# A two-block transformer on one Trainium2 core: a merged attention stage spread over more units, and two weight splits placed earlier

## The chip, the core and the metric

The kernel runs on one core of one Trainium2 chip. The time is device microseconds from start to end of one execution. Before the change three executions took 2884.49, 2887.8 and 2883.33 us; their median is 2884.49 us. The core has a matrix engine (TensorE, PE in the profile), a vector engine (VectorE, DVE), a scalar engine (ScalarE, ACT), GpSimd (POOL) and SyncE (SP), which here only issues transfers. Each engine works through its own instructions in the order in which they are written, and engines wait for each other with semaphores. PSUM, where PE writes, has eight banks of 128 x 512 numbers.

## The reference, cut to what matters

The program is one pass of a network over 512 tokens of width 1024: two attention layers with their feed-forward parts, then a block with a recurrent mixer, a cross attention and a mixture of 32 experts. Three places matter here.

```
# even_mixer: two attentions over the same tokens, 8 heads each
logits = q @ k.T * scale                       # MLA heads, causal
p = softmax(where(mask, logits, -1e30)); out = p @ v
z = q @ k.T * scale                            # stick-breaking heads
log_beta, log_1m = log_sigmoid(z), where(mask, log_sigmoid(-z), 0)
suffix = cumsum_from_the_right(log_1m) - log_1m
a = where(mask, exp(log_beta + suffix), 0); out = a @ v
# hybrid_mixer: proj = xn @ w_in, then for its first 2048 columns
qk = silu(causal_depthwise_conv(qk, conv_w, conv_b))      # 4 taps
# hierarchical_moe, for each block of rows of one expert
hb = silu(xb @ w1[e]) * (xb @ w3[e]); out = hb @ w2[e]
```

## The kernel before

**High and low parts.** The large products take each fp32 number as two: a rounded high part, which ACT writes by a copy (L324; L2319 for the experts), and the rest, which DVE writes by a subtraction (L330; L2324). PE then runs three matmuls for each pair of tiles (L305 to L307, or L2351 to L2353). Weights arrive in a ring of buffers and are split in pieces of 128 x 2048, one ahead of the other; `w_hi` and `x_hi` count ACT's halves, `w_lo` and `x_lo` those of DVE. A piece is written into one of two places (four for the experts), so a split waits until PE has used the piece before in that place.

**The merged attention (stage `two_pe`, `two_act`, `two_dve`, `two_po`).** A unit is one head and one block of 128 queries; its row of scores has 128, 256, 384 or 512 columns (`causal`), and 8 heads give 32 units. Both kinds of attention run their 32 units side by side, one of each per turn of a loop over v. For an MLA unit: scores (L1423), maximum (L974) and its scaling (L1022), exp (L942), transposes of the weights (L897), ACT copy (L925), value product (L907), scaling and store (L952, L954); at two of a head's four units PE also transposes the next head's q or k (L879) and ACT copies it (L918). For a stick unit: scores (L1450), three ACT steps abs, exp and ln (L1478 to L1480, `b_t1`), DVE's softplus (L1515, `b_sp`), a mask on POOL (L1523), DVE's running sum and a subtraction (L1509, L1511, `b_w`), a second mask (L1529), exp (L1485), transposes (L1458), copy (L1492), value product (L1468, `b_o`), and DVE's copy out of the bank (L1499, `b_on`). Only one PSUM bank holds stick value products, so the next one waits for that copy out. A score bank is free again once its unit's subtraction is done (`b_w`). What stands in turn v on each engine, by unit, is written in the loops of the four functions and is the order in which the engines execute.

**The mixer's input (stage `mp_pe`, `mp_act`, `mp_dve`).** PE computes 16 chunks of 128 columns, four per weight matrix (`qkj`); a matrix comes in two pieces. PE first runs all four chunks over piece one, then over piece two. DVE runs the convolution of a chunk in five steps (L1784, L1785, L1787 three times), ACT the silu (L1754). `msp.before` splits a first piece of the next matrix, `msp.after` its second piece: before the change, after the fourth chunk of each matrix.

**The experts (stage `ex_pe`, `ex_act`, `ex_dve`).** 32 experts, each with six pieces of weights (1 MB each). PE multiplies rows with w1 and w3 (`up`), DVE forms the gated product (L2407), PE transposes it (`turn`, L2378), ACT writes the high part (L2413) and DVE the low part (L2417) of the transposed rows, and PE multiplies with w2 (`down`). PE's order is: `up` of the next expert, first half; `turn`; `up`, second half; `down`; `up` with w3. DVE's list for one expert is six piece splits q = p to p+5 with the gated product after the first and the low part (`turned_low`) after the third. SP reloads one of five weight buffers when both splits of its matrix are done (L2669).

Of the kernel before, what the change touches and what calls it, by code (L numbers as in the profile page):

```python
# [33 lines left out]
P = 128  # L34
S = 512
NT = S // P
# [76 lines left out]
def bass_two_blocks_kernel(nc, I, out):  # L113
# [11 lines left out]
    with ctx:  # L125
# [711 lines left out]
        class Attention:  # L837
# [73 lines left out]
            def act(self, act, v):  # L911
                units = self.units
# [6 lines left out]
                if 2 <= v < units + 2:  # L919
                    u = v - 2  # L920
# [5 lines left out]
                if v < units:  # L926
# [243 lines left out]
        if on(1):  # L1170
# [255 lines left out]
            def scale_mla(v):  # L1426
# [5 lines left out]
                            score_banks=(0, 1), turn_banks=(2,), value_banks=(6,), prep_bank=2)  # L1432
# [5 lines left out]
            def sb_bank(v):  # L1438
                return ps[:, 3 + v % 2, 0:causal(v)]
# [4 lines left out]
            def sb_pe(pe, v):  # L1444
                if v < U0:
                    h, i = divmod(v, NT)
                    if v >= 2:
                        pe.wait_ge(b_w, v - 1)
# [3 lines left out]
                if 3 <= v < U0 + 3:  # L1452
                    u = v - 3
# [6 lines left out]
                if 4 <= v < U0 + 4:  # L1460
                    u = v - 4
# [10 lines left out]
            def sb_act(act, ch, v):  # L1472
                if v < U0:
                    act.wait_ge(b_sc, v + 1)
                    if v >= 4:
                        act.wait_ge(b_w, v - 3)
                    t1 = T1[:, v % 4, 0:causal(v)]
                    ch(act.activation(t1, sb_bank(v), ACT.Abs))  # L1478
                    ch(act.activation(t1, t1, ACT.Exp, scale=-1.0))
                    act.activation(t1, t1, ACT.Ln, bias=1.0).then_inc(b_t1, 1)  # L1480
                if 2 <= v < U0 + 2:
                    u = v - 2
# [3 lines left out]
                if 3 <= v < U0 + 3:  # L1486
                    u = v - 3
# [1242 lines left out]
```

## Time and profile before

| | value |
|---|---|
| median of three executions | 2884.49 us (2883.33 to 2887.8) |
| the profiled execution | 2887.3 us, its span 2885.6 us |
| PE busy | 2657.8 us (92%) |
| DVE busy | 1522.2 us (53%) |
| ACT busy | 1234.1 us (43%) |
| POOL busy | 122.6 us (4%) |
| TensorE clock granted, mean | 0.939 |
| DMA | 432.84 MB, mean 150 GB/s |

Busy shares are over the whole span, and the span consists of stages that follow one another. The merged attention lies at 144 to 311 us, the mixer's input at about 1453 to 1605 us, the experts at about 2240 to 2847 us. A row of the timeline gives the start, the length, the engine, the line, the operation, what is written and read, the shapes, the count, and in square brackets the idle time before it with the instruction that ended it. Neighbouring rows of an engine overlap by some 0.1 us where nothing has to be waited for, so times are taken from start to start. A clock of 1.00 is 2.4 GHz, 0.50 is 1.2 GHz.

### The profile page before, as it was taken

What the parts mean: (1) busy time and instruction counts of PE and PEld (TensorE: products, weight loads), DVE (VectorE), ACT (ScalarE), POOL (GpSimd) and SP (SyncE); (2) the same over time, 40 slices, a digit from 0 to 9 for tenths busy, and PEclk for the clock granted to TensorE, in tenths of its full rate; (3) what the DMA queues carried; (4) which work ended last, traced back from release to release, by engine and by line L of the source; (5) the groups of instructions that cost most, each with busy time, mean ns of one, the idle gap of its engine ahead of it and who ended that gap; (6) DMA issues with size and microseconds to landing.
All of it is one profiled execution on the core that took longest, in us unless ns stands there. A gap on an engine that the chain in (4) does not pass through costs nothing. (4 is left out here: it accounts for less than half of the span.)

```text
span 2885.6 us, 30599 instructions
## 1 busy us (share of the span) xinstructions
PE 2657.8 (92%) x12110; PEld 2158.0 (75%) x12110; DVE 1522.2 (53%) x2085; ACT 1234.1 (43%) x1570; POOL 122.6 (4%) x166
## 2 busy tenths in 40 slices
PE   6998999999998999999989969798995899999994
PEld 5866778888887777888877658677874777877774
DVE  4555444344323654434466443245346788888884
ACT  3366432223334742213222222324242677777773
POOL 0111000000140000000000000000002000000001
PEclk9967799999998999999989989899997899999997
DMA  3300132433431023342322022221304899999993
GB/s 130 119 1 1 50 120 93 139 109 119 138 110 37 1 76 116 108 146 88 117 88 88 30 95 88 73 88 59 142 14 190 345 392 396 395 396 396 396 392 119
DMA packets 157146, 432.84 MB, mean 150 GB/s; under 512 B 11051, under 2 KB 80838, under 8 KB 144582
## 3 DMA queue, kind: packets, MB, share of 16 engines
q1 hardware_dynamic: 148950, 400.90, 38.1%
q10 hardware_dynamic: 4608, 16.78, 1.4%
q0 software_dynamic: 3440, 13.11, 1.3%
q8 instruction: 102, 1.67, 0.2%
q14 instruction: 46, 0.38, 0.0%
HBM read 383.58 MB, written 47.19 MB: 149 GB/s over the span
## 5 line engine op out<-in xcount | busy, mean ns | idle before, releaser
L307 PE MATMUL ps<-area,area 128*128 128x512 f32 (+1 forms) x1696 | 658.5, 388 | 0.0
L330 DVE TENSOR_TENSOR area<-area,area 128x2048 fp32r<-128x2048 f32 (+4 forms) x161 | 340.5, 2117 | 598.5 <-ACT area L324 598.5
L306 PE MATMUL ps<-area,area 128*128 128x512 f32 (+5 forms) x1432 | 552.0, 385 | 0.0
L324 ACT ACTIVATE area<-area 128x2048 fp32r<-128x2048 f32 (+4 forms) x161 | 284.1, 1767 | 615.6 <-PE ps L307 582.4
L2324 DVE TENSOR_TENSOR area<-area,area 128x2048 fp32r<-128x2048 f32 x192 | 433.9, 2286 | 107.3 <-ACT area L2319 107.3
L305 PE MATMUL ps<-actT_parts,area 128*128 128x512 f32 x968 | 385.4, 398 | 11.6 <-DVE area L330 9.4
L306 PE MATMUL ps<-actT_parts,area 128*128 128x512 f32 x968 | 383.3, 396 | 0.0
L2319 ACT ACTIVATE area<-area 128x2048 fp32r<-128x2048 f32 x192 | 361.0, 1913 | 48.5 <-PE ps L2353 18.4
L307 PEld LDWEIGHTS ps<-area,area 128*128 128x128 f32 x1696 | 320.4, 189 | 68.3
L306 PEld LDWEIGHTS ps<-area,area 128*128 128x128 f32 x1432 | 277.5, 194 | 52.8
L305 PE MATMUL ps<-area,actT_parts 128*128 128x512 f32 (+3 forms) x704 | 274.6, 390 | 39.6 <-DVE area L330 30.8
L305 PE MATMUL ps<-area,area 128*128 128x512 f32 (+2 forms) x728 | 277.4, 381 | 9.3 <-DVE area L694 9.3
L307 PE MATMUL ps<-area,actT_parts 128*128 128x512 f32 (+3 forms) x704 | 274.0, 389 | 0.0
L305 PEld LDWEIGHTS ps<-actT_parts,area 128*128 128x128 f32 x968 | 183.0, 189 | 57.6 <-DVE area L330 10.3
L306 PEld LDWEIGHTS ps<-actT_parts,area 128*128 128x128 f32 x968 | 182.8, 189 | 42.3 <-issue 1.2
L2351 PE MATMUL ps<-area,actT_parts 128*128 128x512 f32 x512 | 205.9, 402 | 0.0
L2353 PE MATMUL ps<-area,actT_parts 128*128 128x512 f32 x512 | 203.4, 397 | 0.0
L2352 PE MATMUL ps<-area,actT_parts 128*128 128x512 f32 x512 | 203.2, 397 | 0.0
L305 PEld LDWEIGHTS ps<-area,actT_parts 128*128 128x128 f32 x704 | 139.7, 198 | 70.3 <-issue 39.1
L305 PEld LDWEIGHTS ps<-area,area 128*128 128x128 f32 x728 | 137.7, 189 | 35.7 <-issue 10.2
L307 PEld LDWEIGHTS ps<-area,actT_parts 128*128 128x128 f32 x704 | 139.7, 198 | 26.7
L907 PE MATMUL ps<-area,area 128*128 128x64 f32 (+1 forms) x624 | 111.3, 313 | 15.9 <-DVE actT L954 9.3
(329 smaller groups left out, 3205.3 us busy)
## 6 DMA issues: line engine op xcount, KB each, us to landing
area<-in_w SPq DMA_DIRECT2D x96, 2048.0 KB, 10.1
area<-in_w_in SPq DMA_DIRECT2D x16, 2048.0 KB, 7.9
area<-in_l_w_gate SPq DMA_DIRECT2D x22, 1024.0 KB, 5.4
area<-in_l_w_up SPq DMA_DIRECT2D x22, 1024.0 KB, 8.0
expert_inputs<-maskz SPq DMA_DIRECT2D x39, 512.0 KB, 8.7
area<-in_l_w_in SPq DMA_DIRECT2D x9, 2048.0 KB, 8.2
area<-expert_inputs SPq DMA_DIRECT2D x32, 512.0 KB, 9.7
expert_rows<-area ACTq DMA_DIRECT2D x32, 512.0 KB, 8.6
```

The lines of the kernel that those rows point to most:

```text
L305: pe.matmul(dst(r), a.h, b.h, start=begin, stop=False)
L306: pe.matmul(dst(r), a.l, b.h, start=False, stop=False)
L307: m = pe.matmul(dst(r), a.h, b.l, start=False, stop=end)
L324: eng.activation(w.h, raw, ACT.Copy).then_inc(w_hi, 1)
L330: dve.tensor_tensor(w.l, raw, w.high_f, ALU.subtract).then_inc(w_lo, 1)
L907: m = pe.matmul(self.value_at(u), self.PT[:, u % 2, j * P:j * P + P], self.values(u, j), start=(j == 0), stop=(j == nb - 1))
L2319: act.activation(w.h, raw, ACT.Copy).then_inc(x_hi, 1)
L2324: dve.tensor_tensor(w.l, raw, w.high_f, ALU.subtract).then_inc(x_lo, 1)
L2351: pe.matmul(dst, a.h, b.h, start=first, stop=False)
L2352: pe.matmul(dst, a.l, b.h, start=False, stop=False)
L2353: return pe.matmul(dst, a.h, b.l, start=False, stop=last)
```

## The change

Three edits.

1. In the merged attention the MLA scores have one bank instead of two, the stick scores three instead of two. The steps of a unit are spread over more turns, and each engine's turn is put in another order. On PE the stick scores are computed one unit ahead, and the stick value product moves to the end of the turn. On DVE the running sum belongs to the unit two turns back and stands first in the turn, the softplus to the unit one turn back, and the copy out of the value bank stands last. On ACT the abs, exp and ln of a unit have other steps between them. POOL's two masks change places.
2. In the mixer's input the second piece of the next matrix is split after the second of four chunks.
3. In the experts the low part of the transposed rows is written after the second of six splits.

```diff
@@ -1429,36 +1436,38 @@
                             lambda h, i: orow[:, i, h * MV:h * MV + MV], scale_mla, preps,
-                            score_banks=(0, 1), turn_banks=(2,), value_banks=(6,), prep_bank=2)
+                            score_banks=(0,), turn_banks=(2,), value_banks=(6,), prep_bank=2)
             def sb_bank(v):
-                return ps[:, 3 + v % 2, 0:causal(v)]
+                return ps[:, (1, 3, 4)[v % 3], 0:causal(v)]
...
-            def sb_pe(pe, v):
+            def sb_scores(pe, v):
                 if v < U0:
                     h, i = divmod(v, NT)
-                    if v >= 2:
-                        pe.wait_ge(b_w, v - 1)
+                    if v >= 3:
+                        pe.wait_ge(b_w, v - 2)
                     r = slice(64 * (h % 2), 64 * (h % 2) + 64)
                     pe.matmul(sb_bank(v), sbq[r, h // 2, i * P:i * P + P], sbk[r, h // 2, 0:causal(v)],
...
-                if 3 <= v < U0 + 3:
-                    u = v - 3
+
+            def sb_turn(pe, u):
+                if 0 <= u < U0:
                     pe.wait_ge(b_ex, u + 1)
                     if u >= 1:
                         pe.wait_ge(b_pe, u)
...
-                if 4 <= v < U0 + 4:
-                    u = v - 4
+
+            def sb_values(pe, u):
+                if 0 <= u < U0:
                     h = u // NT
                     pe.wait_ge(b_pe, u + 1)
                     if u >= 1:
@@ -1469,36 +1478,22 @@
...
-            def sb_act(act, ch, v):
-                if v < U0:
-                    act.wait_ge(b_sc, v + 1)
-                    if v >= 4:
-                        act.wait_ge(b_w, v - 3)
-                    t1 = T1[:, v % 4, 0:causal(v)]
-                    ch(act.activation(t1, sb_bank(v), ACT.Abs))
-                    ch(act.activation(t1, t1, ACT.Exp, scale=-1.0))
-                    act.activation(t1, t1, ACT.Ln, bias=1.0).then_inc(b_t1, 1)
-                if 2 <= v < U0 + 2:
-                    u = v - 2
...
-            def sb_dve(dve, ch, v):
-                if 5 <= v < U0 + 5:
-                    u = v - 5
-                    h, i = divmod(u, NT)
-                    dve.wait_ge(b_o, u + 1)
-                    dve.tensor_copy(orow[:, i, 512 + h * 64:512 + h * 64 + 64], sb_value(u)).then_inc(b_on, 1)
-                if 1 <= v <= U0:
-                    u = v - 1
+            def sb_sums(dve, ch, u):
...
-                if v < U0:
-                    dve.wait_ge(b_t1, v + 1)
-                    t1 = T1[:, v % 4, 0:causal(v)]
-                    dve.scalar_tensor_tensor(out=t1, in0=sb_bank(v), scalar=0.0, in1=t1,
+
+            def sb_logs(dve, u):
+                if 0 <= u < U0:
+                    dve.wait_ge(b_t1, u + 1)
+                    t1 = T1[:, u % 4, 0:causal(u)]
+                    dve.scalar_tensor_tensor(out=t1, in0=sb_bank(u), scalar=0.0, in1=t1,
                                              op0=ALU.max, op1=ALU.add).then_inc(b_sp, 1)
 
+            def sb_out(dve, u):
+                if 0 <= u < U0:
+                    h, i = divmod(u, NT)
+                    dve.wait_ge(b_o, u + 1)
+                    dve.tensor_copy(orow[:, i, 512 + h * 64:512 + h * 64 + 64], sb_value(u)).then_inc(b_on, 1)
...
-                for v in range(U0 + 1):
-                    if v < U0:
-                        dg = T1[:, v % 4, causal(v) - P:causal(v)]
-                        po.wait_ge(b_sp, v + 1)
...
-                    if v >= 1:
-                        u = v - 1
+                for v in range(U0 + 2):
+                    if v >= 2:
+                        u = v - 2
                         dg = Pb2[:, u % 4, causal(u) - P:causal(u)]
                         po.wait_ge(b_w, u + 1)
...
+                    if 1 <= v <= U0:
+                        u = v - 1
+                        dg = T1[:, u % 4, causal(u) - P:causal(u)]
+                        po.wait_ge(b_sp, u + 1)
...
             def two_pe(pe, ch):
-                for v in range(U0 + 4):
-                    sb_pe(pe, v)
+                sb_scores(pe, 0)
+                for v in range(U0 + 5):
+                    sb_turn(pe, v - 4)
+                    sb_scores(pe, v + 1)
                     mla.pe(pe, v)
+                    sb_values(pe, v - 5)
 
             def two_act(act, ch):
                 act.preload_act_table_set("natural_log_exp_and_others")
-                for v in range(U0 + 3):
-                    sb_act(act, ch, v)
-                    mla.act(act, v)
+                for v in range(U0 + 4):
+                    if v < U0:
+                        t1 = T1[:, v % 4, 0:causal(v)]
+                        act.wait_ge(b_sc, v + 1)
+                        if v >= 4:
+                            act.wait_ge(b_w, v - 3)
+                        ch.mark(act.activation(t1, sb_bank(v), ACT.Abs))
+                    at_abs = ch.n
+                    mla.act_copy(act, v - 3)
+                    sb_weights(act, v - 3)
+                    mla.act_preps(act, v)
+                    if v < U0:
+                        ch.wait(at_abs)
+                        ch.mark(act.activation(t1, t1, ACT.Exp, scale=-1.0))
+                    at_exp = ch.n
+                    sb_copy(act, v - 4)
+                    if v < U0:
+                        ch.wait(at_exp)
+                        act.activation(t1, t1, ACT.Ln, bias=1.0).then_inc(b_t1, 1)
+                    mla.act_exp(act, v)
 
             def two_dve(dve, ch):
-                for v in range(U0 + 5):
-                    sb_dve(dve, ch, v)
+                for v in range(U0 + 6):
+                    sb_sums(dve, ch, v - 2)
+                    sb_logs(dve, v - 1)
                     mla.dve(dve, ch, v)
+                    sb_out(dve, v - 5)
             stage(two_pe, two_act, two_dve, two_po)
             norm, split = out_stage(orow, I["l0_w_o"], G_F0)
         late = []
@@ -1753,7 +1779,7 @@
                     act.wait_ge(midv, cv0 + c + 1)
                     act.activation(mqk[:, c, :], acc[:, c % 2, :], ACT.Silu,
                                    bias=cols2[:, CB + c:CB + c + 1]).then_inc(mida, 1)
-                    if c % 4 == 3:
+                    if c % 4 == 1:
                         msp.after(act, at_qk[j])
                     if c == 7:
                         msp.before(act, 2)
@@ -1789,7 +1815,7 @@
                         if s < 3:
                             ch(ins)
                     ins.then_inc(midv, 1)
-                    if c % 4 == 3:
+                    if c % 4 == 1:
                         msp.after(dve, at_qk[j])
                     if c == 7:
                         msp.before(dve, 2)
@@ -2521,7 +2547,7 @@
                             split_low(dve, q)
                         if q == p:
                             gated(dve, n)
-                        if q == p + 2:
+                        if q == p + 1:
                             turned_low(dve, n)
                         if q == p + 4 and n + 2 < NE:
                             cols_low(dve, n + 2)```

PE in the merged attention, one turn of the loop in the middle of a head. Names: `area_67` and `area_66` are the stick queries and keys, `area_93` its weights, `area_94` and `area_68` its transposed weights and values; `area_72`, `area_73` and `area_57`, `area_58`, `area_71` are the same for MLA. Before:

```order
L1450 MATMUL ps<-area_67,area_66 128x512 [waits b_w]
L1458 MATMUL ps<-ident,area_93 128x128 [waits b_pe,b_ex]
L1468 MATMUL ps<-area_68,area_94 128x64 [waits b_on,b_pe]
L1468 MATMUL ps<-area_68,area_94 128x64 x3
L1423 MATMUL ps<-area_73,area_72 128x512 [waits s_pre,s_ex]
L897 MATMUL ps<-ident,area_57 128x128 [waits s_pre,s_pe,s_ex]
L897 MATMUL ps<-ident,area_57 128x128
L907 MATMUL ps<-area_71,area_58 128x64 [waits s_on,s_pe]
```

and now:

```order
L1466 MATMUL ps<-ident,area_93 128x128 [waits b_pe,b_ex]
L1466 MATMUL ps<-ident,area_93 128x128 x3
L1457 MATMUL ps<-area_67,area_66 128x128 [waits b_w]
L1430 MATMUL ps<-area_73,area_72 128x512 [waits s_pre,s_ex]
L897 MATMUL ps<-ident,area_57 128x128 [waits s_pre,s_pe,s_ex]
L897 MATMUL ps<-ident,area_57 128x128
L907 MATMUL ps<-area_71,area_58 128x64 [waits s_on,s_pe]
L1477 MATMUL ps<-area_68,area_94 128x64 [waits b_on,b_pe]
L1477 MATMUL ps<-area_68,area_94 128x64 x2
```

The stick value product, which stood third in the turn, is now its last step, behind all MLA steps, and the stick scores stand second.

DVE in the same stage, from one copy out of the value bank to the next. Before:

```order
L1499 COPY actT<-ps 128x64 [waits b_o]
L1509 SCALAR_TENSOR_TENSOR area_93<-ones,area_95 128x384 [waits b_pt,b_m1]
L1511 TENSOR_TENSOR area_93<-ps,area_93 128x384 [waits vch]
L1515 SCALAR_TENSOR_TENSOR area_95<-ps,area_95 128x512 [waits b_t1]
L952 RECIPROCAL rinv<-rs 128x1 [waits s_ex]
L954 TENSOR_SCALAR actT<-ps,rinv 128x64 [waits s_o,vch]
L974 ISA ps,mx<-ps,maskz 128x512 [waits s_sc]
```

and now:

```order
L1519 COPY actT<-ps 128x64 [waits b_o]
L1504 SCALAR_TENSOR_TENSOR area_93<-ones,area_95 128x384 [waits b_pt,b_m1]
L1506 TENSOR_TENSOR area_93<-ps,area_93 128x384 [waits vch]
L1512 SCALAR_TENSOR_TENSOR area_95<-ps,area_95 128x512 [waits b_t1]
L959 RECIPROCAL rinv<-rs 128x1 [waits s_ex]
L961 TENSOR_SCALAR actT<-ps,rinv 128x64 [waits s_o,vch]
L981 ISA ps,mx<-ps,maskz 128x128 [waits s_sc]
```

DVE's sequence is the same but for the unit of its last row; what changes is which step of PE the first row waits for: the fourth-last step of a turn before, the last step of a turn now.

DVE in the experts, one expert's list (L2324, now L2350, are the splits; L2417, now L2443, the low part of the transposed rows; L2407, now L2433, the gated product). Before:

```order
L2324 TENSOR_TENSOR area_10612<-area_132,area_10611 128x2048 [waits x_hi]
L2407 TENSOR_TENSOR area_136<-area_135,ps 128x512 [waits m_tr,m_si,x_use]
L2324 TENSOR_TENSOR area_127<-area_50,area_126 128x2048 [waits x_hi]
L2324 TENSOR_TENSOR area_10640<-area_50,area_10639 128x2048 [waits x_hi]
L2417 TENSOR_TENSOR area_138<-ps,area_137 128x512 [waits m_hh]
```

and now:

```order
L2350 TENSOR_TENSOR area_10612<-area_132,area_10611 128x2048 [waits x_hi]
L2433 TENSOR_TENSOR area_136<-area_135,ps 128x512 [waits m_tr,m_si,x_use]
L2350 TENSOR_TENSOR area_127<-area_50,area_126 128x2048 [waits x_hi]
L2443 TENSOR_TENSOR area_138<-ps,area_137 128x512 [waits m_hh]
L2350 TENSOR_TENSOR area_10640<-area_50,area_10639 128x2048 [waits x_hi]
```

The low part moved ahead of one split; nothing else of the list did.

## Rows read from the trace of the kernel before

**Rows 1.** Stretches: us, busy us of each engine (instructions), PE clock, DMA share, GB/s

```profile
200.00:290.00 90.00, 81.61 (x367) 59.80 (x366) 51.63 (x162) 60.32 (x152) 9.41 (x36) 0.73 0.00 1
2300.00:2800.00 500.00, 492.20 (x2257) 397.94 (x2256) 423.22 (x269) 384.25 (x323) 0.00 (x0) 1.00 1.00 395
```

**Rows 2.** Waits, merged attention, 144 to 310 us: total us, times, longest

```profile
DVE area L1515 <- ACT area L1480: 57.3, 25, 3.3
```

**Rows 3.** Timeline, DVE: the same step of two successive heads

```profile
255.98 0.21 DVE L1499 COPY actT<-ps 128x64 f32<-128x64 f32 x1
...
276.12 0.21 DVE L1499 COPY actT<-ps 128x64 f32<-128x64 f32 x1
```

**Rows 4.** Timeline, PE: a turn at the full clock

```profile
271.90 0.91 PE L1450 MATMUL ps<-area,area 64*128 64x384 f32 x2
...
272.74 0.66 PE L1458 MATMUL ps<-ident,area 128*128 128x128 f32 x4
...
273.24 0.78 PE L1468 MATMUL ps<-area,area 128*128 128x64 f32 x6
...
273.85 0.60 PE L879 MATMUL ps<-ident,area 128*96 128x128 f32 x4
...
274.29 0.81 PE L1423 MATMUL ps<-area,area 96*128 96x384 f32 x2
```

**Rows 5.** Timeline, PE: the same steps at half the clock

```profile
292.36 1.65 PE L1450 MATMUL ps<-area,area 64*128 64x384 f32 x2
293.94 1.11 PE L1458 MATMUL ps<-ident,area 128*128 128x128 f32 x4
294.84 1.38 PE L1468 MATMUL ps<-area,area 128*128 128x64 f32 x6
296.02 1.59 PE L1423 MATMUL ps<-area,area 96*128 96x384 f32 x2
```

**Rows 6.** DVE lines of the stick units: duration ns min/median/max

```profile
L1509 DVE TENSOR_TENSOR_SCAN area<-ones,area x32: 410/814/1216, 148.3 to 306.3; 128x128 f32<-128x128 f32 x8, 128x256 f32<-128x256 f32 x8, 128x384 f32<-128x384 f32 x8, 128x512 f32<-128x512 f32 x8
L1511 DVE TENSOR_TENSOR area<-ps,area x32: 291/490/692, 148.7 to 307.6; 128x128 f32<-128x128 f32 x8, 128x256 f32<-128x256 f32 x8, 128x384 f32<-128x384 f32 x8, 128x512 f32<-128x512 f32 x8
```

**Rows 7.** Timeline, mixer input: ACT's second silu and late split, DVE's split, PE

```profile
1472.84 0.72 ACT L1754 ACTIVATE area<-area,cols 128x512 f32<-128x512 f32 x1 [2.75 <-DVE area L1787]
...
1480.43 2.04 ACT L324 ACTIVATE area<-area 128x2048 fp32r<-128x2048 f32 x2
```

**Rows 8.** Timeline, mixer input, PE around its two waits

```profile
1484.70 0.80 PE L305 MATMUL ps<-actT_parts,area 128*128 128x512 f32 x1 [8.41 <-DVE area L330]
...
1489.93 0.39 PE L305 MATMUL ps<-actT_parts,area 128*128 128x512 f32 x1
...
1549.88 0.50 PE L305 MATMUL ps<-actT_parts,area 128*128 128x512 f32 x1 [1.01 <-DVE area L330]
```

**Rows 9.** Timeline, one expert: ACT's and DVE's part of the transposed rows, and PE

```profile
2505.57 0.60 ACT L2413 ACTIVATE area<-ps 128x512 fp32r<-128x512 f32 x1 [1.31 <-PE ps L2378]
...
2507.89 0.68 DVE L2417 TENSOR_TENSOR area<-ps,area 128x512 fp32r<-128x512 f32 x1
2507.94 0.40 PE L2353 MATMUL ps<-area,actT_parts 128*128 128x512 f32 x1
...
2508.97 0.40 PE L2352 MATMUL ps<-area,area 128*128 128x512 f32 x1
...
2509.20 0.39 PE L2353 MATMUL ps<-area,area 128*128 128x512 f32 x1
```

**Rows 10.** Who waited for L2417, whole run: us, times

```profile
  PEld ps L2351: 23.4, 31
```

**Rows 11.** The issuing line, 2804 to 2812 us: the last weight transfer, time to landing

```profile
L2669 SPq DMA_DIRECT2D area<-in_w x1: 328/328/328, 2806.1 to 2806.1; - x1
...
DMA to landing us min/median/max: 9.2/9.2/9.2
```

**Rows 12.** Timeline, ACT: the split that first reads that transfer

```profile
2828.53 1.92 ACT L2319 ACTIVATE area<-area 128x2048 fp32r<-128x2048 f32 x1 [1.47 <-PE ps L2353]
```

More of the change, by code:

```diff
@@ L911, in act, with act_preps @@
             def act(self, act, v):
-                units = self.units
+                self.act_preps(act, v)
+                self.act_copy(act, v - 2)
+                self.act_exp(act, v)
+            def act_preps(self, act, v):
                 for n, (at, done, _, d, gain) in enumerate(self.preps):
@@ L918, in act, with act_copy @@
                         act.activation(d, ps[0:d.shape[0], self.prep_bank, :], ACT.Copy, scale=gain).then_inc(s_pre, 1)
-                if 2 <= v < units + 2:
-                    u = v - 2
+            def act_copy(self, act, u):
+                if 0 <= u < self.units:
                     act.wait_ge(s_pt, self.pt0 + u + 1)
@@ L925, in act, with act_exp @@
                     act.activation(self.PT[:, u % 2, 0:L], self.turned(u, 0, L), ACT.Copy).then_inc(s_pe, 1)
-                if v < units:
+            def act_exp(self, act, v):
+                if v < self.units:
                     L = self.length(v)
@@ L1485, in sb_act, with sb_copy @@
                     act.activation(p, p, ACT.Exp).then_inc(b_ex, 1)
-                if 3 <= v < U0 + 3:
-                    u = v - 3
+            def sb_copy(act, u):
+                if 0 <= u < U0:
                     L = causal(u)
@@ L1530, in two_po @@
                                          base=0, pattern=[[-1, P]], channel_multiplier=1).then_inc(b_m2, 1)
+                    if 1 <= v <= U0:
+                        u = v - 1
+                        dg = T1[:, u % 4, causal(u) - P:causal(u)]
+                        po.wait_ge(b_sp, u + 1)
+                        po.affine_select(out=dg, in_=dg, compare_op=ALU.is_gt, fill=0.0,
+                                         base=0, pattern=[[-1, P]], channel_multiplier=1).then_inc(b_m1, 1)
             def two_pe(pe, ch):
-                for v in range(U0 + 4):
-                    sb_pe(pe, v)
+                sb_scores(pe, 0)
+                for v in range(U0 + 5):
+                    sb_turn(pe, v - 4)
+                    sb_scores(pe, v + 1)
                     mla.pe(pe, v)
+                    sb_values(pe, v - 5)
             def two_act(act, ch):
                 act.preload_act_table_set("natural_log_exp_and_others")
-                for v in range(U0 + 3):
-                    sb_act(act, ch, v)
-                    mla.act(act, v)
+                for v in range(U0 + 4):
[18 more added lines that the diff above has]
+                    mla.act_exp(act, v)
             def two_dve(dve, ch):
-                for v in range(U0 + 5):
-                    sb_dve(dve, ch, v)
+                for v in range(U0 + 6):
+                    sb_sums(dve, ch, v - 2)
+                    sb_logs(dve, v - 1)
                     mla.dve(dve, ch, v)
+                    sb_out(dve, v - 5)
             stage(two_pe, two_act, two_dve, two_po)
```

7 lines of the change are left out of this document (4 added, 3 removed).

## The prediction, made before the changed kernel ran

> **What bounds the kernel now.** I read the table of stretches first, then the waits, then the timeline of a head, a weight matrix and an expert; the stages follow one another, so each edit is priced in its own stage.
>
> In the merged attention no engine is full: in 90 us DVE is busy 51.6 and ACT 60.3 us, PE 81.6 us, and PE had a mean granted clock of 0.73, so it spent about 46% of the time at 2.4 GHz and the rest at 1.2 GHz [rows 1]. DVE's longest wait is for ACT's ln (57.3 us in 25 times) [rows 2]: ln, softplus, maximum, MLA exp, the next unit's abs, exp and ln follow one another across two engines. A head of both kinds takes 276.12 - 255.98 = 20.14 us [rows 3]. In the mixer's input PE is the bound but for two waits on a split. In the experts PE is busy 492 of 500 us, and the DMA share is 1.00 at 395 GB/s [rows 1]: two resources near their limit.
>
> **Merged attention: the loop that the new order makes.** The old alternation of ln and MLA exp goes: ln and MLA exp now stand side by side on ACT, and the softplus and the maximum are a turn apart. What is late next can be read in the code. DVE's turn v ends with the copy out of the value bank of unit v-5, which waits for PE's last step of turn v. DVE's turn v+1 begins with the sum and the subtraction of unit v-1. PE's turn v+1 may do the transposes of unit v-3, and then its stick scores, of unit v+2, wait for that subtraction: their bank, one of three, is the bank of unit v-1. The third bank gives no slack, since the scores went one unit forward and the sum one turn back. So from the last value product to the next stick scores PE has only a unit's transposes, and DVE does nothing else than copy, sum, subtraction. Before, the value product was the third step of a turn, and the copy was long ready.
>
> The price of this loop for one head, 10 blocks of 128 columns. PE at the full clock, start to start [rows 4]: scores 0.84 us for three blocks, 0.28 a block; transposes 0.50 for four, 0.125; values 0.61 for three, 0.203; a prep (q or k of the next head) 0.44. In the loop lie both scores, MLA's transposes, both value products and two preps: 10 x (0.56 + 0.125 + 0.406) + 0.88 = 11.8 us. At half the clock [rows 5]: 1.58 / 3 = 0.527, 0.90 / 4 = 0.225, 1.18 / 3 = 0.393, a prep twice 0.44: 10 x (1.054 + 0.225 + 0.786) + 1.76 = 22.4 us. DVE: the copy 0.21 [rows 3], the sum 0.81 and the subtraction 0.49 as medians of the four lengths [rows 6], four of each: 6.0 us, and some 0.4 us for handing over twice a unit. A head: 18.2 us at the full clock, 28.8 us at half. ACT (60.3 us in 90, or 13.5 a head [rows 1, 3]) and DVE (11.6) stay below that.
>
> With the clock's two levels shared as before (46% and 54% of the time), a head takes 1 / (0.46 / 18.2 + 0.54 / 28.8) = 22.7 us, 2.6 us more than now. The loop is closed for about seven of the eight heads: 7 x 2.6 = 18 us **lost**. Bounds: all at the full clock, 8 x (18.2 - 20.14) = -16 us; all at half, 8 x (28.8 - 20.14) = +69 us. I take +18, the value for the clock that the rows show in this stage. It can hardly rise, since PE's own work at the full clock (13.1 us a head with the stick transposes) fills 72% of 18.2 us, while now it pauses less.
>
> **Mixer input.** PE stood idle 8.41 us and started again at 1484.70, at half the clock [rows 8]. It waited for the second piece of the second matrix, whose split stood behind four convolutions: ACT began it at 1480.43 and DVE needed the time to 1484.70 after that, 4.27 us [rows 7, 8]. Now ACT starts it after the second silu, which began at 1472.84 and lasts 0.63 as far as the next start; the place for the piece had been free since the first matrix was done. So 1473.47 + 4.27 = 1477.74: PE waits some 1.5 us and starts 6.96 us earlier. A pause of 1.01 us later in this stage was followed at once by matmuls of the full-clock length [rows 8], so I expect no fall of the clock; the twelve matmuls from 1484.70 to 1489.93 took 5.23 us and would take 12 x 0.23 = 2.8 (0.23 from the steps in [rows 9]): 2.4 us more. The same edit at the fourth matrix removes the wait before 1549.88, whose loss is 1.2 us with the slow start. Two convolutions per matrix (3.5 us each) are now behind the split. They are covered: after each of these matrices PE has its next one or the narrow gates product to do, 10 us and more, and the PSUM banks that it takes next are those of convolutions done by then. At the last matrix DVE finishes some 7 us later, with two matrices of PE work still ahead. Sum: -7.0 - 2.4 - 1.2 = **-10.6 us**; bounds -12 and -5 (if the clock falls in the short pause).
>
> **Experts.** ACT's high part of the transposed rows was ready at 2505.57 + 0.60 = 2506.17, DVE wrote the low part from 2507.89 to 2508.57, since a third split stood before it, and PE had to wait: from 2507.94 to 2508.97 it started two matmuls where its step is 0.23, a loss of 1.03 - 0.46 = 0.57 us [rows 9]. The weight loads of L2351 waited so 31 times, 23.4 us in all [rows 10]. Now the low part starts at 2506.2, is done at 2506.9, 1.3 us before PE wants it. The third split slips by 1.1 us, to about 2509.1; PE needs its piece after one more half product and a row transpose, near 2511.8. So 31 x 0.57 = 17.7 us of PE time goes, unless transfers end last. The last weights landed at 2806.1 + 9.2 = 2815.3 and were first read at 2828.53 [rows 11, 12]: 13.2 us of lead. If the transfers can't be speeded up at all (share 1.00), that lead is used up and bounds the gain at 13.2 us; they have perhaps 2 us in them, since faster splits issue them sooner. I take **-15.5 us**; bounds -18 and 0.
>
> The Trainium skill's page "DMA: Bandwidth & Descriptors" (section "Where 436 GB/s comes from") puts the ceiling of the ports at 435 GB/s, against our 395. By it the transfers could follow PE, and the gain would be the whole 17.7 us; by the DMA share in [rows 1] they are full. No run yet shows which.
>
> **Sum.** +18 - 10.6 - 15.5 = -8 us. The profiled execution took 2887.3 us, 1.7 more than its span and 2.8 us above the median of the three; so 2879 for it and **2877 us** against the median. A measurement of this kernel can tell 0.2%, 5.8 us: faster means below 2878.7, slower above 2890.3.
>
> **Rivals.**
> *The clock follows the new pauses (slower).* In the new loop PE pauses once a unit for copy, sum and subtraction (1.5 us less the transposes). If the full-clock share of the stage falls from 46% to 15%, a head takes 1 / (0.15 / 18.2 + 0.85 / 28.8) = 26.5 us, 7 x 6.4 = 45 us lost: 2887.3 + 45 - 26.1 - 2.8 = 2903 us. It decides from a share of about 33% (24.2 us a head, +29), where the sum passes zero. For: 46% is all that PE holds now with fewer pauses [rows 1]. Against: at half the clock the loop keeps PE busy 25 of 28.8 us a head, so the clock has cause to come back.
> *The loop doesn't bind and the stage gains.* If PE holds the full clock throughout, the stage gains 16 us instead of losing: 2843 us. For: the wait that cost DVE 57.3 us is gone [rows 2]. Against: the same loop exists at either clock.
> *The transfers are the bound in the experts.* The lead of 13.2 us can't be used, because with every place reloaded earlier nothing lands earlier and the queue only waits elsewhere; gain 2 us instead of 15.5: 2890 us. For: share 1.00. Against: landed weights lie unused for 13 us.
>
> **How the numbers follow.** Forecast 50%, the clock rival 23%, the stage that gains 12%, the transfers 12%, the rest 3%. The forecast's own range is 2866 to 2888 (the share of the clock 40 to 52%, experts 13 to 18). Half of it and a bit more (0.30) is faster, 0.17 within, 0.03 slower; the gaining stage adds 0.12 to faster; the transfers split 0.02, 0.05 and 0.05; the clock rival 0.02 within and 0.21 slower. That gives 0.45, 0.25 and 0.30. For 8 in 10 the range runs from 2850 to 2908.
>
> **What would show it.** DVE's copy out of the value bank waits for the stick value product in nearly every unit, and the stick scores wait for the subtraction; heads of 22 to 23 us; a stage 18 us longer, at a clock near 0.73. PE's pause in the mixer's input near 1.5 us. No wait for the low part of the transposed rows, and experts every 18.05 us, or 18.2 with ACT waiting for transfers near the end. The forecast is wrong if that copy doesn't wait, if the clock of the attention leaves 0.65 to 0.8, or if the expert's step stays at 18.6.

## The result, and the profile after: slower by 0.74%

The changed kernel takes 2910.95 us (median of 8 runs, 2900.43 to 2914.52), the kernel before 2886.59 us in the same comparison (8 runs): ratio 1.0074, interval 1.0064 to 1.0085. Forecast were 2877 us and a range up to 2908: wrong in sign, and 3 us outside the range. The profiled execution took 2914.38 us with a span of 2912.6 us and a mean granted clock of 0.923; before, 2887.3, 2885.6 and 0.939.

Three steps of the program, found in both traces, cut the span into parts:

| part (from the first and last starts of a line) | before | after | difference |
|---|---|---|---|
| start to the last copy out of the stick value bank | 318.8 | 371.3 | +52.5 us |
| from there to the first L2351 / L2377 of the experts | 1928.8 | 1920.0 | -8.8 us |
| first to last L2351 / L2377 | 588.1 | 571.1 | -17.0 us |

Two edits gave about what was forecast (-10.6 and -15.5). The merged attention lost 52.5 us where +18 was forecast.

**The clock of the merged attention.** The table of stretches after (length, busy time of PE, PEld, DVE, ACT and POOL, PE clock, DMA share, GB/s); the third row is the stretch of [rows 1], 0.73 before:

```profile
144.00:170.00 26.00, 19.59 (x52) 10.60 (x51) 11.04 (x32) 12.63 (x35) 2.56 (x9) 0.50 0.00 0
170.00:200.00 30.00, 25.84 (x87) 17.81 (x85) 11.87 (x36) 13.04 (x35) 2.22 (x8) 0.50 0.00 1
200.00:290.00 90.00, 76.12 (x282) 52.71 (x281) 38.60 (x120) 42.34 (x115) 7.35 (x26) 0.58 0.00 1
144.00:372.00 228.00, 190.71 (x666) 132.97 (x665) 95.02 (x288) 100.83 (x271) 18.14 (x64) 0.54 0.00 1
```

Over the whole stage the mean is 0.54: 8% of the time at 2.4 GHz, the rest at 1.2. Before, the same row for 144 to 320 us reads 0.68, 36%: the 46% that the prediction took from the middle of the stage was above the stage's own share.

**The loop.** What the changed kernel's copy-out (L1519, L1499 before) waited for:

```profile
L1519 DVE COPY actT<-ps x32: 224/225/225, 173.6 to 371.3; 128x64 f32<-128x64 f32 x32
its engine sat idle before it (us, times) until:
  PE ps L1477: 55.8, 31
```

On VectorE's (DVE's) timeline, the same copy-out in two successive heads, which answers to [rows 3], and what follows it:

```profile
211.05 0.23 DVE L1519 COPY actT<-ps 128x64 f32<-128x64 f32 x1 [1.79 <-PE ps L1477]
...
240.44 0.22 DVE L1519 COPY actT<-ps 128x64 f32<-128x64 f32 x1 [1.79 <-PE ps L1477]
240.59 0.68 DVE L1504 TENSOR_TENSOR_SCAN area<-ones,area 128x256 f32<-128x256 f32 x1
241.30 0.42 DVE L1506 TENSOR_TENSOR area<-ps,area 128x256 f32<-128x256 f32 x1
```

and TensorE (PE) in the same turn, its last value product, the transposes, and the scores that wait for the subtraction at 241.30:

```profile
239.35 1.06 PE L1477 MATMUL ps<-area,area 128*128 128x64 f32 x4
240.20 1.06 PE L1466 MATMUL ps<-ident,area 128*128 128x128 f32 x4
241.78 0.79 PE L1457 MATMUL ps<-area,area 64*128 64x128 f32 x2 [0.52 <-DVE area L1506]
```

This is the loop of the prediction, link by link: value product, copy-out, sum, subtraction, scores. The copy-out, which waited three times before (4.0 us), now waits 31 times, 55.8 us. A head at half the clock takes 240.44 - 211.05 = 29.4 us; forecast were 28.8. The six heads from the fourth copy-out on take 29.4, 29.4, 22.1, 29.4, 29.4 and 24.4 us; in the third the clock was full for a while. The wait of [rows 2], 57.3 us for ACT's ln, is gone as expected: on its line (L1512) DVE no longer stands idle. It was exchanged for the copy-out's 55.8 us.

**Mixer and experts.** TensorE's one wait for a split in the mixer's input, 1440 to 1680 us of the changed kernel (total us, times, longest):

```profile
PE ps L305 <- DVE area L330: 1.5, 1, 1.5
```

The same on its timeline, which answers to [rows 8]:

```profile
1530.70 0.50 PE L305 MATMUL ps<-actT_parts,area 128*128 128x512 f32 x1 [1.47 <-DVE area L330]
```

8.41 us became 1.47 us (forecast 1.5), the matmuls behind it start 0.23 us apart after the first, so at the full clock, and the wait of 1.01 us is gone. In the experts, ScalarE's (ACT's) high part in two successive experts, on its timeline [rows 9]:

```profile
2542.44 0.60 ACT L2439 ACTIVATE area<-ps 128x512 fp32r<-128x512 f32 x1 [1.31 <-PE ps L2404]
...
2560.51 0.60 ACT L2439 ACTIVATE area<-ps 128x512 fp32r<-128x512 f32 x1 [1.31 <-PE ps L2404]
```

DVE's low part of the first of them:

```profile
2543.07 0.69 DVE L2443 TENSOR_TENSOR area<-ps,area 128x512 fp32r<-128x512 f32 x1 [0.43 <-ACT area L2439]
```

And the stretch 2400 to 2800 us:

```profile
2400.00:2800.00 400.00, 400.00 (x1860) 329.67 (x1859) 349.54 (x222) 316.94 (x266) 0.00 (x0) 1.00 1.00 407
```

DVE now comes to the low part before ACT's high part is written, and waits for it in all 32 experts (15.3 us in all; before once, 1.5 us). PE's matmuls waited for the low part 62 times, 33.5 us, before, and wait for it twice now, 3.0 us. PE is busy in 400.00 of 400 us, and an expert takes 18.07 us (forecast 18.05). The DMA moved 407 GB/s where it moved 395 [rows 1], so a share of 1.00 was no bound there. The last weight transfer was issued at 2835.2 and landed 8.1 us later; ACT first read it at 2855.30, so the lead is still 12.0 us where it was 13.2 [rows 11, 12].

### The profile page after: what moved, and what is told of

It is laid out like the page before. It is cut to its first block and busy times, and to the rows that moved or that the text cites. A ratio compares the mean times of both kernels' runs of the same rounds, so it can differ in the third digit from the quotient of the medians.

```text
span 2912.6 us, 30600 instructions
## 1 busy us (share of the span) xinstructions
PE 2682.0 (92%) x12110; PEld 2179.3 (75%) x12110; DVE 1523.5 (52%) x2085; ACT 1225.5 (42%) x1570; POOL 122.5 (4%) x166
## 5 line engine op out<-in xcount | busy, mean ns | idle before, releaser
L330 DVE TENSOR_TENSOR area<-area,area 128x2048 fp32r<-128x2048 f32 (+4 forms) x161 | 340.6, 2117 | 599.1 <-ACT area L324 599.1
L324 ACT ACTIVATE area<-area 128x2048 fp32r<-128x2048 f32 (+4 forms) x161 | 284.2, 1767 | 606.1 <-PE ps L307 574.5
L2350 DVE TENSOR_TENSOR area<-area,area 128x2048 fp32r<-128x2048 f32 x192 | 433.2, 2284 | 76.9 <-ACT area L2345 76.9
L305 PE MATMUL ps<-actT_parts,area 128*128 128x512 f32 x968 | 383.8, 396 | 3.7 <-DVE area L802 2.2
L305 PE MATMUL ps<-area,actT_parts 128*128 128x512 f32 (+3 forms) x704 | 275.0, 391 | 39.9 <-DVE area L330 30.8
L305 PE MATMUL ps<-area,area 128*128 128x512 f32 (+2 forms) x728 | 277.3, 381 | 8.7 <-DVE area L694 8.7
L305 PEld LDWEIGHTS ps<-actT_parts,area 128*128 128x128 f32 x968 | 182.3, 188 | 48.9 <-DVE area L802 3.1
L2378 PE MATMUL ps<-area,actT_parts 128*128 128x512 f32 x512 | 203.0, 396 | 0.0
L305 PEld LDWEIGHTS ps<-area,actT_parts 128*128 128x128 f32 x704 | 140.6, 200 | 70.6 <-issue 39.3
L305 PEld LDWEIGHTS ps<-area,area 128*128 128x128 f32 x728 | 137.7, 189 | 35.0 <-issue 9.6
L907 PE MATMUL ps<-area,area 128*128 128x64 f32 (+1 forms) x624 | 116.7, 326 | 9.6 <-DVE actT L1019 6.1
```

The costliest lines, as they stand in the source:

```text
L305: pe.matmul(dst(r), a.h, b.h, start=begin, stop=False)
L324: eng.activation(w.h, raw, ACT.Copy).then_inc(w_hi, 1)
L330: dve.tensor_tensor(w.l, raw, w.high_f, ALU.subtract).then_inc(w_lo, 1)
L907: m = pe.matmul(self.value_at(u), self.PT[:, u % 2, j * P:j * P + P], self.values(u, j), start=(j == 0), stop=(j == nb - 1))
L2350: dve.tensor_tensor(w.l, raw, w.high_f, ALU.subtract).then_inc(x_lo, 1)
L2378: pe.matmul(dst, a.l, b.h, start=False, stop=False)
```

## The experiments

Line numbers in the rows are those of each kernel: where lines were added, L1519 reads L1521, L1477 L1479. Rows of stretches have the columns named above. Every run is compared with runs of the kernel before on the same chip. The medians of the kernel before in these comparisons are 2886.6 (the result), 2885.9, 2886.8 and 2885.0 us, so that times of different groups can be set side by side to some 2 us.

### One edit at a time

Each kernel holds the named edit alone, as it stands in the diff of the change; for `mix_alone` for instance

```diff
-                    if c % 4 == 3:
+                    if c % 4 == 1:
                         msp.after(act, at_qk[j])
```

(the same on DVE), for `exp_alone` only `q == p + 1`, for `mix_exp` both of these, for `att_alone` all the rest.

> The attention edit alone; the mixer's and the experts' splits stand where they stood before. Theory of the sum: the three edits act apart, and the merged attention stage alone costs the 52.5 us by which its last copy-out (163.8 to 318.8 us before, 173.6 to 371.3 us after) now ends later, so 2886.6 + 52 = about 2938 us (2932 to 2945). In the trace: TensorE's granted clock at 0.50 in nearly all of the stage, a head of 29.4 us at that level, and 33 us of TensorE waits of the experts' matmuls for VectorE's low parts back again. Rival, the edits share something (the level of the clock is carried into later stages, or transfers that start later land in another stage): the sum fails, and this one stands by 5 us or more away from 2938 us.

Measured 2935.0 us (2930.26 to 2938.83; ratio 1.0171, 1.0155 to 1.0187). The clock was not at 0.50 in nearly all of the stage: it was at 0.65 between 200 and 290 us, and two heads took 22.06 us where the changed kernel has one.

> The mixer edit alone on the kernel before: both attn-free splits are issued after the second chunk of each four instead of after the fourth. Theory of the sum: 9.2 us less (from the last attention copy-out to the experts' first matmul the kernel before takes 1928.8 us, the changed kernel 1920.0 us, and the wait of TensorE for VectorE's split there fell from 9.4 to 1.5 us), so 2886.6 - 9.2 = about 2877 us (2874 to 2880). Rival, the gain in that stretch belongs to other transfers or clock levels behind the longer attention stage: 2884 us or more.

Measured 2876.09 us (2873.42 to 2883.91; 0.9967, 0.9956 to 0.9979).

> The expert edit alone on the kernel before: the low part of the turned activations is made one split sooner. Theory of the sum: 17 us less (from the first to the last first-product matmul of the experts 588.1 us before, 571.1 us after; TensorE's waits for that low part fell from 33.5 us, 62 times, to 3.0 us, twice), so 2886.6 - 17.0 = about 2870 us (2866 to 2873), with 403 to 408 GB/s in the expert stage. Rival, transfers bind as soon as TensorE's waits go: the weights land as before at 395 GB/s and the gain is 10 us or less, 2877 us or more.

Measured 2869.86 us (2866.61 to 2876.62; 0.9945, 0.9929 to 0.9961).

> The mixer edit and the expert edit together on the kernel before, without the attention edit. Theory of the sum: 2886.6 - 9.2 - 17.0 = about 2860 us (2856 to 2865), the fastest of the four. Rival, the two gains overlap (both take the same lead of the transfers over TensorE, so that the second gives less behind the first): 2866 us or more.

Measured 2859.48 us (2857.55 to 2866.64; 0.9911, 0.9895 to 0.9926).

The sum holds within 3 us each time: against 2885.9 the attention costs 49, the mixer gives 9.8, the experts 16.1, both together 26.5. No gain is carried between stages. The transfers' rival falls with `exp_alone`, whose stretch of the experts reads

```profile
2350.00:2800.00 450.00, 450.00 (x2093) 370.89 (x2092) 392.67 (x250) 356.07 (x299) 0.00 (x0) 1.00 1.00 406
```

All of the loss lies in the attention. What follows takes it apart.

### Cutting the loop, on one engine or the other

```diff
-                    sb_out(dve, v - 5)
+                    sb_out(dve, v - 6)
```

> The changed kernel with one number changed: VectorE copies the stick value bank out at the end of the turn after (unit v-6 in turn v, not v-5), so that it waits for a product that TensorE finished a turn ago. Theory A (the loop, and the clock that follows it): the loop from TensorE's last step over copy-out, sum and subtraction to the next stick scores is cut; the 55.8 us of waits for the copy-out go, TensorE has fewer pauses, and its clock shares the two levels again as before; a head takes 18 to 21 us (23 to 25 us where the clock is at half), the stage 160 to 190 us instead of 228 us, the whole 2848 to 2875 us. Theory B (the new order itself is what is long: one mla score bank, steps of ScalarE interleaved with the chain): another wait takes the place of the copy-out, VectorE then waits for ScalarE's logarithm or TensorE's mla scores as long, a head at half clock stays above 28 us, the whole stays at 2900 to 2915 us. Theory C (the clock's level doesn't follow the pauses): heads at half clock all through, 23.5 to 25.5 us each, the whole about 2870 to 2880 us with the clock at 0.50 in the entire stage.

Measured 2886.56 us (12 runs, 2871.35 to 2891.92; 0.9997, 0.9986 to 1.0009).

```diff
                     sb_turn(pe, v - 4)
+                    sb_values(pe, v - 5)
                     sb_scores(pe, v + 1)
                     mla.pe(pe, v)
-                    sb_values(pe, v - 5)
```

> The changed kernel with the same loop cut on the other engine: TensorE does the stick value products right after the turns, ahead of the stick scores, not as the last step of its turn; VectorE's order is the changed kernel's. Theory A: as with the later copy-out, the loop is cut, 2848 to 2875 us, and the wait of the copy-out for the value product falls from 55.8 us to under 10 us. Theory B: 2900 to 2915 us. Theory C: 2870 to 2885 us, clock 0.50 all through the stage.

Measured 2879.73 us (12 runs, 2871.65 to 2885.36; 0.9969, 0.9956 to 0.9982).

The loop was there and cost time: one number gives 24 us back, the other order of PE 31. Theory B falls. The copy-out's waits of 55.8 us became, in `out_late`,

```profile
its engine sat idle before it (us, times) until:
  PE ps L1477: 2.3, 2
```

In `val_early` they became 4.8 us in 3 times. But theory A expected the clock to come back with the pauses gone, and it didn't: 0.54 in 200 to 290 us of `out_late`, 0.60 in `val_early`. (The profiled run of `out_late` is the fastest of its 12, with a mean clock of 0.937; the others have 0.927 to 0.933.) Three heads at half the clock, each the stretch from a copy-out to the fourth after it, show what the loop is worth by itself. The old order, in `mix_alone`:

```profile
163.10:188.20 25.10, 24.91 (x86) 17.95 (x85) 11.76 (x38) 13.93 (x34) 2.15 (x8) 0.50 0.00 1
```

The changed kernel:

```profile
211.05:240.44 29.39, 25.22 (x86) 17.60 (x85) 11.88 (x36) 12.53 (x35) 2.27 (x8) 0.50 0.00 1
```

`out_late`:

```profile
221.40:247.17 25.77, 25.18 (x86) 17.69 (x85) 11.49 (x37) 12.62 (x34) 2.25 (x8) 0.50 0.00 1
```

PE has the same 25 us of work in each; the loop adds 4.2 us of pauses, and without it PE is full. So theory C's time for `out_late` (2870 to 2880) is nearer than A's, but its reason isn't shown: these runs don't say whether the level follows the pauses. The next two ask just that.

### Filling the pauses with work that nobody needs

```diff
                         pe.wait_ge(b_pe, u)
+                    for _ in range(5):
+                        pe.matmul(ps[:, 5, 0:P], ident[:, :], ident[:, :], start=True, stop=True)
                     for j in range(causal(u) // P):
```

> The changed kernel, loop and all, with five products of the identity by itself (128x128, into the turn bank ahead of the turns that write over them) in each turn of TensorE's stick turns, 160 in all; their results are not used. They stand where TensorE waits for the subtraction, and are work that the stage doesn't need. Theory A (the clock follows TensorE's pauses): the pauses filled, the clock goes to its full level and stays, a head takes 18 to 20 us as the loop gives at full clock, the stage 160 to 175 us instead of 228 us, the whole 2843 to 2870 us: more work, less time. Theory C (the level doesn't follow the pauses): the clock stays at 0.50, the five products cost 5 x 0.43 us a turn against about 1 us of pause, a head takes 33 to 35 us, the whole 2935 to 2960 us.

Measured 2859.6 us (2855.58 to 2861.2; 0.9902, 0.9885 to 0.9919): 160 additional products make the changed kernel 51 us faster. The stretch of [rows 1], and one head in it:

```profile
200.00:290.00 90.00, 81.01 (x552) 63.46 (x551) 54.26 (x162) 53.91 (x152) 10.14 (x36) 1.00 0.00 1
225.97:246.23 20.26, 18.33 (x126) 14.29 (x126) 11.88 (x36) 12.28 (x35) 2.25 (x8) 1.00 0.01 2
```

The clock stays at 1.00, and a head takes 20.26 us instead of 29.39, though the loop is still closed (the copy-out still waits 28.0 us in 25 times). Theory C falls: the level follows what PE does. Whether it is the filled pauses, the greater amount of work or its kind (plain products of 128 columns among transposes and products of 64) is not shown by this run.

The same in the old order, with the mixer and expert edits, four products between `sb_pe(pe, v)` and `mla.pe(pe, v)`, into free columns of bank 7:

> The kernel before with the mixer edit and the expert edit, and in the old merged attention four products of the identity by itself in each turn between TensorE's stick steps and its mla steps (112 in all, results not used). Theory A (the clock follows TensorE's pauses): the clock stays at its full level, a head takes about 19 to 20 us all through instead of 19.6 to 23.4 us, and the whole is 10 to 20 us under the same kernel without them, about 2840 to 2852 us. Theory C: the clock alternates as before and the four products cost up to 4 x 0.43 us a turn wherever it is at half: 2870 us or more.

Measured 2846.76 us (2844.44 to 2847.58; 0.9858, 0.9838 to 0.9877), 12.7 us under `mix_exp`. Its stretch:

```profile
200.00:290.00 90.00, 84.37 (x558) 65.33 (x558) 55.59 (x175) 66.45 (x164) 10.24 (x38) 1.00 0.01 1
```

So part of the time of the kernel before was this clock as well: its heads of 19.6 to 21 us become 18.9.

### How much filling, and which order is better at the full clock

`fill3` is `fill5` with 3 for 5; `outlate_fill2` and `outlate_fill3` are `out_late` with 2 and 3 products a turn; `mixexp_fill2` is `mixexp_fill4` with 2.

> The changed kernel, loop and all, with three unused products a turn in place of five, 96 in all. Five kept the clock at 1.00 with a head of 20.3 us, in which TensorE still waited 1.3 us for the subtraction. If three keep the clock too, the head is that of the loop alone at full clock, 18.2 us by the sum in the prediction (18 to 19), and the whole 2859.6 - 7 x 1.8 = about 2847 us (2842 to 2853). If they do not, the clock falls back to half in most of the stage: 2885 to 2930 us, above what no products at all would lead one to fear, since each product then costs twice as much.

Measured 2870.17 us, and runs far apart: 2854.39 to 2886.01 (0.9930, 0.9908 to 0.9952). The six runs of this one program, with the granted clock of each:

```
us     2854.39  2858.51  2869.84  2870.50  2874.14  2886.01
clock    0.957    0.957    0.950    0.950    0.947    0.944
```

With three products the level alternates, and not alike in every run. Two stretches of the profiled one, the slowest:

```profile
232.00:262.00 30.00, 27.20 (x120) 20.77 (x119) 14.06 (x43) 14.36 (x41) 2.25 (x8) 0.66 0.00 1
262.00:285.00 23.00, 19.96 (x134) 15.49 (x135) 13.89 (x44) 14.00 (x41) 2.84 (x10) 1.00 0.00 1
```

Neither "kept" nor "not kept" was right. The instructions are the same in every run; of what is recorded only the clock differs, and the time goes with it.

> The changed kernel with the later copy-out (unit v-6 in turn v) and two unused products of the identity in each of TensorE's stick turns, 64 in all. The clock theory, if two suffice: clock 1.00 through the stage, and, with the loop cut, a head under the 18.9 us of the old order with four products and the 20.3 us of the changed one with five: about 17 us; against the 2859.6 us with five products and the loop that is some 6.5 heads x 3.3 us less, 2838 us (2832 to 2846). If two do not suffice, the clock alternates or stays at half with heads of up to 25.8 us + 4 x 2 x 0.5 us, and the whole is 2865 to 2900 us. Rival, the old order is as good once the clock is full: not under the 2846.8 us of the old order with four products.

Measured 2854.92 us (median of 5, 2850.57 to 2910.84; ratio 0.9891, 0.9875 to 0.9907, without the longest run). The run of 2910.84 us had a mean clock of 0.928, the four others 0.950 to 0.952.

> The same with three unused products a turn, 96 in all. If the clock is full either way, the third costs TensorE 4 x 0.27 us of a head and up to half of it shows: a head of about 17.4 us, the whole 2841 us (2835 to 2848). If two are too few and three enough, this one is the fastest and the other above 2865 us.

Measured 2847.85 us (2845.12 to 2848.98; 0.9866, 0.9851 to 0.9880).

> The kernel before with the mixer edit, the expert edit and two unused products a turn in place of four in the old merged attention, 56 in all. If two keep the clock full: a head of 18.3 to 18.9 us, the whole 2842 to 2847 us. If not: alternating levels as without products, 2855 to 2868 us.

Measured 2844.51 us (2841.68 to 2849.33; 0.9859, 0.9843 to 0.9876).

One head of `outlate_fill2` on VectorE's timeline (a copy-out and the fourth after it):

```profile
226.94 0.21 DVE L1521 COPY actT<-ps 128x64 f32<-128x64 f32 x1
...
244.64 0.21 DVE L1521 COPY actT<-ps 128x64 f32<-128x64 f32 x1
```

and one of `mixexp_fill2`:

```profile
240.40 0.21 DVE L1499 COPY actT<-ps 128x64 f32<-128x64 f32 x1
...
258.67 0.21 DVE L1499 COPY actT<-ps 128x64 f32<-128x64 f32 x1
```

17.70 us against 18.27: at the full clock and with two products each, the new order without its loop is the better one, by 0.6 us a head. It isn't the faster kernel, because it starts later. Its first stick value product starts at 171.3 us, that of `mixexp_fill2` at 160.7, and its clock was late to rise besides (mean 0.59 in its first head, 26.05 us from 178.64). The last value product starts at 310.4 against 301.3 us. With three products the first starts at 170.2 us and the last at 300.8: the clock is full in time, but the third product costs the head what the order gave (18.6 us). How much of the late start lies in the order and how much in the clock was not taken apart.

I had expected 2838 us for `outlate_fill2`, and the rival of that run was right: not under 2846.8. For `outlate_fill3` the time is within the forecast (2835 to 2848), but its head was to take 17.4 us, and the other one was not above 2865. `mixexp_fill2` came out as expected in time, but its heads take 18.3 and 19.2 us in turn and the first 20.6, where 18.3 to 18.9 were expected: its clock is 0.98 between 200 and 290 us, not quite full.

The fastest are the old order with two or four products, 2844.5 and 2846.8 us, and the new order without its loop and with three, 2847.9 us. Their ratios to the kernel before, 0.9859, 0.9858 and 0.9866, have intervals that overlap, so these runs don't tell them apart. All three beat the kernel before by 1.3 to 1.4%, and the median of the changed one is 2.2 to 2.3% above them.

## Why the prediction was wrong, point by point

- **The loop** (copy-out behind PE's last step, then sum, subtraction, scores): right in mechanism, and in size at half the clock, 29.4 us against 28.8 forecast. Moving the copy-out, or the value product, shows it as a cause: -24 and -31 us. At the full clock it was sized too small. `fill3` has a head at a clock of 1.00 with the loop closed:

```profile
217.42:237.07 19.65, 16.62 (x110) 12.50 (x110) 11.87 (x36) 12.16 (x35) 2.25 (x8) 1.00 0.00 1
```

That is 19.65 us, where 18.2 were forecast. The three unused products seem to cost nothing in it: the second and third of its four copy-outs follow after 5.18 and 3.98 us, and in the changed kernel, which has no such products, the same two follow after 5.18 and 3.97 us in a place where its clock was full:

```profile
261.11:270.26 9.15, 7.36 (x43) 4.78 (x41) 5.41 (x18) 5.76 (x15) 1.14 (x4) 1.00 0.01 3
```

With 19.65 and 29.4 us, and the clock shared as forecast, a head would take 23.9 us and the term would be some +26 instead of +18 us, an estimate.

- **The step that failed: "With the clock's two levels shared as before (46% and 54% of the time)".** The share of the full clock was 16% in the stretch from which I took the 46%, and 8% in the stage, and +18 us became +52.5. The prediction had named the sign: it is wrong if the clock of the attention leaves 0.65 to 0.8. Bounds of -16 and +69 for this term were honest at the upper end, but I let the value in their middle stand on a clock that the same edit changes.
- **Where the 52.5 us lie.** The six full heads from the fourth copy-out on took 27.3 us on average instead of 21.0: 38.2 us. The last four copy-outs take 12.6 us in both. The other 14.3 us were lost before the fourth copy-out:

```profile
180.31 0.21 DVE L1499 COPY actT<-ps 128x64 f32<-128x64 f32 x1
194.65 0.23 DVE L1519 COPY actT<-ps 128x64 f32<-128x64 f32 x1 [2.49 <-PE ps L1477]
```

The prediction put nothing for this start of the stage. There the copy-out stands later in its turn than before, and the stick scores wait for the subtraction even before there is a copy-out:

```profile
157.54 0.79 PE L1457 MATMUL ps<-area,area 64*128 64x128 f32 x2 [1.81 <-DVE area L1506]
```

No run takes this part by itself. By the prediction's formula with 8% and 29.4 us, a head takes 28 us, and 7 x (28 - 20.14) = 55 us. That this is near 52.5 is luck in part: it has too much for each head and nothing for the start.

- **The rival that took its place**, the clock that follows the new pauses, was priced at 2903 us for a share of 15% and given 23%. What I held against it, that PE's 25 busy microseconds of 28.8 at half the clock give it cause to come back, is refuted: PE was busy 25.22 of 29.39 us and the level stayed. Even 25.18 of 25.77 us in `out_late` ran wholly at 0.50. What I should have weighed is the other level. In the kernel before, heads of 20 us at mixed levels already let the clock fall time and again, without the loop's pauses; these come on top. With those pauses filled (`fill5`: PE busy 18.33 of 20.26 us) the clock held.
- **Mixer**: -10.6 forecast, -9.8 alone. **Experts**: -15.5 forecast, -16.1 alone; the transfers gained 12 GB/s and kept 12.0 us of lead. Of the two readings of [rows 1] that the prediction weighed, the one by the DMA share is refuted: 407 GB/s, above the 395 that I had read as full. The other goes by the ceiling of 435 GB/s on the Trainium skill's page "DMA: Bandwidth & Descriptors" (section "Where 436 GB/s comes from"). This trace agrees with it, since 407 GB/s lie under that ceiling; no run here reached it.
- **The rival that the stage gains** at the full clock (2843 us): with the measured 19.65 us a head it would have been 8 x (19.65 - 20.14) = -4 us and some 2854 us, an estimate; the shortest run of `fill3` took 2854.39 us. Its time is nearly reached by `mixexp_fill2` and `outlate_fill3`, but those have no such loop.

Open: whether the products help by filling pauses, by the amount of work or by its kind (they can't be told apart here, since plain products were always put where PE paused), and why the level, once low, stays low for so long in `out_late` although PE is busy nearly throughout. That the clock was at half already in the first 26 us of the stage, before the loop closes, was seen in both orders and not tested.

## What to carry to other kernels

When an edit puts pauses into a TensorE that runs at an alternating clock, price the stage at both levels and don't take the old share of them for the new one: the clock is a result of the edit. Where a stage waits on a chain of other engines and its clock sits low, a few products that nobody needs, placed where PE waits, can be worth more than a better order; try two or three amounts, since too few leave a kernel whose time scatters by 1%. And when an order is rotated, follow each engine's last step of a turn to the next turn's first: a copy-out there ties two engines together; moving it a turn later was one number, and gave 24 us.

## What the runs showed of the hardware, and I had not expected

- The clock didn't come back with PE busy: 25.18 of 25.77 us, and still 0.50. In the kernel before the same holds for 282.8 to 306.3 us:

```profile
282.80:306.30 23.50, 23.32 (x78) 16.72 (x78) 11.80 (x38) 12.60 (x32) 2.15 (x8) 0.50 0.00 1
```

- One program's time can scatter by 1.1% (`fill3`, 2854.39 to 2886.01 us at mean clocks of 0.957 to 0.944) with the clock as the only difference that the records show.
- A DMA share of 1.00 stood at 395 GB/s and at 407 GB/s: the share says that transfers are queued, not how fast they could go.
